# Retention products of three heads from fp32 to three fp32r passes, with split values and split decayed scores

## The chip, the cores and the metric

The kernel runs on one core of a Trainium2 chip. The metric is the device time of one execution in microseconds (us), the median of several runs. The engines are named as in the profile: PE is TensorE (matmuls), PEld its weight loads, DVE is VectorE, ACT is ScalarE, POOL is GpSimd, and SP issues most of the DMAs.

## The reference

Two transformer blocks one after the other, on 256 tokens of x and 256 of a context, width 1024. The first block's first layer is the one that matters here, retention with 4 heads (key width 256, value width 512), forwards and backwards. It is a scan over chunks of 128 tokens:

```
def step(r, qkv):
    qc, kc, vc = qkv
    s = einsum('bhid,bhjd->bhij', qc, kc) * dmask
    o = einsum('bhij,bhjv->bhiv', s, vc) + einsum('bhid,bhdv->bhiv', qc, r) * xi
    r = r * chunk_decay + einsum('bhjd,bhjv->bhdv', kc * zeta, vc)
    return r, o
...
ox_f, _ = retention_scan(qx, kx, vx, lg_f, rc_f)
ox_b, _ = retention_scan(flip(qx), flip(kx), flip(vx), lg_b, rc_b)
y = silu(gf) * head_norm(of) + silu(gb) * head_norm(ob)
return y @ w_out
```

All is float32. After it come a gated convolutional FFN, a layer of differential attention with another FFN, and a second block (two kinds of attention, a recurrent branch, an MLP).

## The kernel before

**Dense steps.** Nearly all of PE's work is weights times activations at nearly fp32 precision. A weight unit is 128 x 1024 numbers; four units (j = 0 to 3) make a step. SP loads a unit into `raw`; ScalarE copies it as fp32r into `wh` (L1619), VectorE makes `wl` = raw - wh (L2415), and PE runs three fp32r passes for each product, high x high, high x low and low x high (`three`, L615 to L617). A step is 4 units of 8 products of 512 columns, so 24 passes a unit. PE frees a unit by `unit_used`; ScalarE waits for that before it writes the next high part there. The results stand in half of PSUM (`main`, banks 0 to 3, or `side`, banks 4 to 7).

**Retention.** The scan is unrolled: all 512 tokens at once, four key tiles of 128. For each head h there are four dense steps, in this order: qk (queries and keys), v (values), gf and gb (the gates of both directions). Other work is hosted between the units of these steps, in the half of PSUM that the step does not use:
- v step: the queries and keys are turned (L921). At its end both engines copy the values to `vres`, ScalarE banks 0 and 1 (L1872) and VectorE banks 2 and 3 (L2788).
- gf step (here called the decay step): the scores (`score_tiles`, L930), tiles 0 to 2 after unit 0 and tile 3 after unit 1. VectorE multiplies them with decay factors from PSUM into `pf` and `pb`, forward and backward, 1280 columns each (`decay`, L2731).
- gb step: the forward products, decayed scores times values (`attend`, L937), 7 after unit 0 and 3 after unit 1.
- qk step of the next head: the backward products, also 7 and 3. (For the last head they lie between the first units of the output projection.)

Each `attend` is followed by ScalarE's squares (`rms_attended`, L1816, L1819) and VectorE's gate (`gate`, L2741 to L2749), and the next `attend` of the same direction waits for `gated`, since it writes the same banks. `silu_gate` (L1839) takes the gates out of PSUM at the end of gf and gb steps.

**Order.** Each engine's program is written out by hand, in the order in which it runs, and joined by semaphores. `close()` on VectorE waits for ScalarE's `act_evac` and then issues a tiny memset (L2437) that counts `emptied`: the half of PSUM is free. Between all this VectorE does `sum_slot` (L2477, L2479), the sums of modulation weights that POOL loads.

**Memory.** `pf` and `pb` lie in the arena at 32 and 37 kB, the turned queries and keys `qkt` at 42 to 50 kB, the decay factors `dec` at 58 to 62 kB. `ah` and `al` are the high and low activations for later projections; nothing uses them before the last head's retention.

Of the kernel before, what the change touches and what calls it, by code (L numbers as in the profile page):

```python
# [8 lines left out]
ALU = mybir.AluOpType  # L9
# [3 lines left out]
F32R = mybir.dt.float32r  # L13
# [170 lines left out]
def build(nc, a, out):  # L184
    ctx = ExitStack()
    with ctx:
        def sb(name, shape, dt=F32):
            return ctx.enter_context(nc.sbuf_tensor(name, shape, dt))

        def sem(name):  # L190
            return ctx.enter_context(nc.semaphore(name))
# [32 lines left out]
        spare = sb("spare", [1, 1])  # L224
        ARENA = 79 * 256
        arena = sb("arena", [P, ARENA])
        ps = ctx.enter_context(nc.psum_tensor("ps", [P, 8, 512], F32))

        def area(kb, *shape):

            n = int(np.prod(shape))
            o = int(kb * 256)
            assert o + n <= ARENA, (kb, shape)
            v = arena[:, o:o + n]
            if len(shape) == 1:
                return v
            names = "abcd"[:len(shape)]
            return v.rearrange(f"p ({' '.join(names)}) -> p {' '.join(names)}",
                               **dict(zip(names[1:], shape[1:])))
# [3 lines left out]
        qk = area(32, 4, 512)  # L243
        pf, pb = area(32, 1280), area(37, 1280)
        qkt = area(42, 4, 512)
        rtmp = area(42, 512)
        sgb = area(50, 4, 512)
        dec = area(58, 2, 512)
# [148 lines left out]
        y_rms, y_gated, h_done = sem("y_rms"), sem("y_gated"), sem("h_done")  # L397
        qkt_turned, qkt_act, qkt_vec = sem("qkt_turned"), sem("qkt_act"), sem("qkt_vec")
        scored, decayed = sem("scored"), sem("decayed")
        attended, gate_rms, gated = sem("attended"), sem("gate_rms"), sem("gated")  # L400
        y_turned, yt_act, yt_vec = sem("y_turned"), sem("yt_act"), sem("yt_vec")
        ada_summed, ada_added, mods_kept = sem("ada_summed"), sem("ada_added"), sem("mods_kept")
# [199 lines left out]
        def _(pe):  # L602
# [330 lines left out]
            def attend(v0, reads, tiles, half):  # L933

                for t in tiles:
                    for n, (c, k) in enumerate(reads[t]):
                        mm = pe.matmul(ps[:, half + t % 2, :], v0[:, c:c + P], vres[:, k, :],  # L937
                                       start=n == 0, stop=n == len(reads[t]) - 1)
                mm.then_inc(attended, 1)

            def turn_y(pair, half):

                for f in range(4):
                    for t in range(2):
                        c = (f % 2) * SEQ + t * P
                        mm = pe.transpose(ps[:, half + f // 2, c:c + P], sgf[:, 2 * pair + t, f * P:(f + 1) * P], ident[:, :])
                mm.then_inc(y_turned, 1)
# [11 lines left out]
            for h in range(RH):  # L959
                d = 4 * h  # L960
                dense = G.now() if h else 6
                if h:
                    mods_emptied(2 * h - 2)
                    pe.wait_ge(gated, 4 * h - 2)
                    for j in dense_tokens(main):
                        if j == 0:
                            pe.wait_ge(emptied, dense)
                            attend(pb, BWD_READS, (0, 1), side)
                        elif j == 1:
                            pe.wait_ge(gated, 4 * h - 1)  # L970
                            attend(pb, BWD_READS, (2, 3), side)
                        elif j == 2:
                            turn_y(0, side + 2)
                if h:
                    y_taken(2 * h - 1)
                    pe.wait_ge(gated, 4 * h)
                else:
                    pe.wait_ge(ada_taken, 4)
                    pe.wait_ge(emptied, 6)
                for j in dense_tokens(side):  # L980
                    if j == 0:
                        pe.wait_ge(emptied, dense + 1)
                        if h:
                            turn_y(1, main)
                    elif j == 1:
                        if h:
                            y_taken(2 * h)
                        pe.wait_ge(qk_rot, h + 1)
                        turn_q(h, 0, main)
                    elif j == 2:  # L990
                        qkt_taken(2 * h + 1)
                        turn_q(h, 1, main)
                    host_mods(d + 1, j, main)
                if h:
                    mods_emptied(2 * h - 1)
                qkt_taken(2 * h + 2)
                for j in dense_tokens(main):
                    if j == 0:
                        pe.wait_ge(emptied, dense + 2)
                        score_tiles((0, 1, 2), side)  # L1000
                    elif j == 1:
                        pe.wait_ge(decayed, 3 * h + 1)
                        score_tiles((3,), side)
                pe.wait_ge(decayed, 3 * h + 3)
                for j in dense_tokens(side):
                    if j == 0:
                        pe.wait_ge(emptied, dense + 3)
                    host_mods(d + 3, j, main)
                    if j == 0:
                        attend(pf, FWD_READS, (0, 1), main)  # L1010
                    elif j == 1:
                        pe.wait_ge(gated, 4 * h + 1)
                        attend(pf, FWD_READS, (2, 3), main)


            def project_rows(half, part):
# [586 lines left out]
        def _(act):  # L1603
# [238 lines left out]
            for h in range(RH):  # L1842
                def ahead(units):
                    split(units=units) if h < RH - 1 else split_rows(0, 0, units)

                if h:
                    silu_gate(sgb)
                    split(units=range(3, 4))
                    split(units=range(0, 1))
                    rms_attended(4 * h - 2, side)  # L1850
                    split(units=range(1, 2))
                    rms_attended(4 * h - 1, side)
                    split(units=range(2, 3))
                    take_y(2 * h - 2, side + 2)
                hb = step_full()
                T.mark(act.activation(qk[:, 2:4, :], ps[:, hb + 2:hb + 4, :], ACT.Copy), act_evac)
                split(units=range(3, 4))
                for z in range(2):
                    T.mark(act.activation(dec[:, z, :], kdist[:, z, :], ACT.Exp,
                                          scale=lgt[:, 4, h + 4 * z:h + 4 * z + 1]), (act_own, decay_exp)[z])  # L1860
                split(units=range(0, 1))
                if h:
                    take_y(2 * h - 1, main)
                    keep_mods(2 * h - 1, main)
                split(units=range(1, 2))
                take_qkt(2 * h, main)
                split(units=range(2, 3))
                take_qkt(2 * h + 1, main)
                if 2 * h - 1 in GATES:
                    keep_gate(2 * h - 1, main)  # L1870
                hb = step_full()
                T.mark(act.activation(vres[:, 0:2, :], ps[:, hb:hb + 2, :], ACT.Copy), act_evac)  # L1872
                split(units=range(3, 4))
                split(units=range(0, 3))
                silu_gate(sgf)
                split(units=range(3, 4))
                ahead(range(0, 1))
                keep_mods(2 * h, main)
                rms_attended(4 * h, main)
                ahead(range(1, 2))  # L1880
                rms_attended(4 * h + 1, main)
                ahead(range(2, 3))
                if 2 * h in GATES:
                    keep_gate(2 * h, main)
# [519 lines left out]
        def _(vec):  # L2404
# [15 lines left out]
            def step_full():  # L2420
                half = 4 * (par.base % 2)
                par.next()
                T.settle()
                vec.wait_ge(unit_used, S.next() * SLOTS + SLOTS)
                return half
# [13 lines left out]
            def act_read():  # L2439

                vec.wait_ge(act_evac, E.next() + 1)

            def close():

                act_read()
                tick(emptied)
# [35 lines left out]
            def sum_slot(d, j):  # L2482


                if 0 < d < 15:
                    sum_unit(4 * (d - 1) + j)
# [266 lines left out]
            for h in range(RH):  # L2753
# [31 lines left out]
                split(units=range(2, 3))  # L2785
                sum_slot(d + 1, 3)
                hb = step_full()
                T.mark(vec.tensor_copy(vres[:, 2:4, :], ps[:, hb + 2:hb + 4, :]), vec_own)  # L2788
                close()
                split(units=range(3, 4))  # L2790
                sum_slot(d + 2, 0)
                split(units=range(0, 1))
# [8 lines left out]
                sum_slot(d + 2, 2)  # L2801
                split(units=range(2, 3))
                sum_slot(d + 2, 3)
                step_full()
                close()
                split(units=range(3, 4))
# [805 lines left out]
```

## Time and profile before

| | |
|---|---|
| median of 3 runs | 1842.75 us (1841.95 to 1844.41) |
| the profiled execution | 1843.4 us, span 1841.3 us |
| granted clock, mean over the span | 0.992 |
| PE busy | 1789.2 us, 97% |
| VectorE busy | 1149.2 us, 62% |
| ScalarE busy | 837.7 us, 45% |
| DMA | 282.38 MB, mean 153 GB/s |

The span runs from the first to the last instruction; the execution's own time is a little longer. A busy share is an average over stages that have different limits. A matmul's record lasts longer than its slot in the stream, because matmuls overlap; the distance of two starts tells what one costs. The retention stage lies between about 60 and 520 us.

### The profile page before, as it was taken

How to read it: one execution, taken by the hardware profiler on the slowest of the kernel's cores; microseconds unless marked ns; L12 is line 12 of the kernel's file. 1: busy time of each engine (PE TensorE's matmuls, PEld its weight loads, DVE VectorE, ACT ScalarE, POOL GpSimd, SP SyncE). 2: the span in 40 equal slices, each digit the busy share in tenths (PEclk: the TensorE clock that was granted, in tenths of full speed). 3: DMA queues.
4: the chain of work that ended last, by engine and by line, in shares of the span. 5: the costliest groups of instructions: out<-in, count | busy, mean ns of one | idle time of the engine just before them, and what ended most of it. 6: DMA issues, size and time to landing. Idle time of an engine off the chain costs nothing. (4 is left out here: it accounts for less than half of the span.)

```text
span 1841.3 us, 26290 instructions
## 1 busy us (share of the span) xinstructions
PE 1789.2 (97%) x9881; PEld 1499.7 (81%) x9881; DVE 1149.2 (62%) x1539; ACT 837.7 (45%) x1216; POOL 85.4 (5%) x160
## 2 busy tenths in 40 slices
PE   7999999999999999999999998899999999989998
PEld 6877868778678888888878887799879987879987
DVE  4766667667267688644346566666665695765555
ACT  5334233241456432233345556566554646544454
POOL 3010101100000010000000000000001000000000
PEclk9999999999999999999999999999999999999999
DMA  9644545545265476432323222455546454536664
GB/s 333 207 134 147 167 142 157 154 125 174 85 225 184 132 233 184 127 105 81 114 68 104 81 81 81 139 181 182 192 141 209 148 165 144 188 126 194 182 194 126
DMA packets 153229, 282.38 MB, mean 153 GB/s; under 512 B 12795, under 2 KB 82547, under 8 KB 153008
## 3 DMA queue, kind: packets, MB, share of 16 engines
q1 hardware_dynamic: 136496, 223.69, 38.5%
q0 software_dynamic: 16640, 57.42, 10.3%
q8 instruction: 63, 1.03, 0.2%
q14 instruction: 30, 0.25, 0.0%
HBM read 276.83 MB, written 4.23 MB: 153 GB/s over the span
## 5 line engine op out<-in xcount | busy, mean ns | idle before, releaser
L2415 DVE TENSOR_TENSOR wl<-raw,wh 128x1024 fp32r<-128x1024 f32 (+1 forms) x388 | 455.1, 1181 | 377.2 <-ACT wh L1619 374.7
L1619 ACT ACTIVATE wh<-raw 128x1024 fp32r<-128x1024 f32 (+1 forms) x388 | 394.2, 1022 | 610.3 <-PE ps L617 603.2
L615 PE MATMUL ps<-uh,wh 128*128 128x256 f32 (+1 forms) x1216 | 382.2, 314 | 7.0 <-DVE spare L2437 7.0
L616 PE MATMUL ps<-ul,wh 128*128 128x256 f32 (+1 forms) x1216 | 380.2, 313 | 0.0
L617 PE MATMUL ps<-uh,wl 128*128 128x256 f32 (+1 forms) x1216 | 379.9, 312 | 0.0
L615 PE MATMUL ps<-wh,uh 128*128 128x512 f32 (+2 forms) x960 | 367.2, 382 | 7.1 <-issue 6.2
L616 PE MATMUL ps<-wl,uh 128*128 128x512 f32 (+2 forms) x960 | 353.5, 368 | 0.0
L617 PE MATMUL ps<-wh,ul 128*128 128x512 f32 (+2 forms) x960 | 353.3, 368 | 0.0
L615 PEld LDWEIGHTS ps<-uh,wh 128*128 128x128 f32 x1216 | 232.9, 192 | 22.4 <-issue 6.6
L617 PEld LDWEIGHTS ps<-uh,wl 128*128 128x128 f32 x1216 | 232.9, 192 | 12.5
L616 PEld LDWEIGHTS ps<-ul,wh 128*128 128x128 f32 x1216 | 233.0, 192 | 12.3
L615 PE MATMUL ps<-wh,ah 128*128 128x512 f32 x584 | 229.3, 393 | 0.6 <-DVE al L2550 0.4
L617 PE MATMUL ps<-wh,al 128*128 128x512 f32 x584 | 227.4, 389 | 0.0
L616 PE MATMUL ps<-wl,ah 128*128 128x512 f32 x584 | 227.3, 389 | 0.0
L615 PEld LDWEIGHTS ps<-wh,uh 128*128 128x128 f32 x960 | 182.1, 190 | 51.4 <-issue 20.3
L616 PEld LDWEIGHTS ps<-wl,uh 128*128 128x128 f32 x960 | 182.1, 190 | 33.3 <-issue 5.3
L617 PEld LDWEIGHTS ps<-wh,ul 128*128 128x128 f32 x960 | 181.7, 189 | 30.6
L2477 DVE SCALAR_TENSOR_TENSOR arena<-arena,cvec 128x1024 f32<-128x1024 f32 x140 | 173.6, 1281 | 8.4 <-DVE res L2749 0.5
L615 PEld LDWEIGHTS ps<-wh,ah 128*128 128x128 f32 x584 | 109.6, 188 | 26.0 <-issue 3.2
L617 PEld LDWEIGHTS ps<-wh,al 128*128 128x128 f32 x584 | 109.6, 188 | 22.9
L616 PEld LDWEIGHTS ps<-wl,ah 128*128 128x128 f32 x584 | 109.7, 188 | 22.7 <-issue 0.5
L937 PE MATMUL ps<-res,arena 128*128 128x512 f32 x160 | 72.5, 600 | 3.0 <-DVE res L2749 2.1
(315 smaller groups left out, 1491.5 us busy)
## 6 DMA issues: line engine op xcount, KB each, us to landing
raw<-in_ffn_w_up SPq DMA_DIRECT2D x176, 256.0 KB
arena<-in_ada_w POOLq DMA_DIRECT2D x80, 512.0 KB, 4.2
raw<-in_w_in SPq DMA_DIRECT2D x60, 512.0 KB
raw<-in_ret_w_in SPq DMA_DIRECT2D x48, 512.0 KB
raw<-in_ffn_w_down SPq DMA_DIRECT2D x40, 512.0 KB
raw<-in_ret_w_out SPq DMA_DIRECT2D x32, 512.0 KB
raw<-in_w_up SPq DMA_DIRECT2D x32, 512.0 KB
raw<-in_w_down SPq DMA_DIRECT2D x32, 512.0 KB
```

Of the source, the lines that this page charges most:

```text
L615: pe.matmul(o, lh, rh, start=first, stop=False)
L616: pe.matmul(o, lh, rl, start=False, stop=False)
L617: return pe.matmul(o, ll, rh, start=False, stop=last)
L937: mm = pe.matmul(ps[:, half + t % 2, :], v0[:, c:c + P], vres[:, k, :], start=n == 0, stop=n == len(reads[t]) - 1)
L1619: T.mark(act.activation(wh[:, j, 0:size], raw[:, j, 0:size], ACT.Copy), hi_done)
L2415: T.mark(vec.tensor_tensor(wl[:, j, 0:size], raw[:, j, 0:size], wh[:, j, 0:size], ALU.subtract), lo_done)
L2477: ins = vec.scalar_tensor_tensor(out=o, in0=w, scalar=c32[:, k, c:c + 1], in1=o, op0=ALU.mult, op1=ALU.add)
```

## The change

For heads 0 to 2 the values and the decayed scores are kept as a high part (fp32r) and a low part (the rest, as fp32r), and each product of `attend` becomes three fp32r passes (`attend_split`). Head 3 keeps the fp32 products, since `ah` and `al` are needed for the projection by then.

- Values: ScalarE writes the high part of all four banks to `ah` in two copies, VectorE subtracts twice into `al`. The copy to `vres` goes.
- Decayed scores: after the last decay ScalarE copies `pf` to `pfh` (1280 columns) and `pb` to `pbh` (768 and 512), between the high parts of units 1 and 2; VectorE subtracts in place to `pfl` and `pbl`, after its last sums and before the `close()` of the gf step. `pfh` and `pbh` lie where `qkt` and one half of `dec` have been.
- Four semaphores are new: v_high, v_low, p_high, p_low.

```diff
+        arena0 = nc.sbuf_base - 4 * ARENA
+        def split_area(name, kb, n):
+            return nc.alloc_sbuf_tensor_at(name, [P, n], F32R, offset=arena0 + 1024 * kb)
...
+        pfl, pbl = split_area("pfl", 32, 1280), split_area("pbl", 37, 1280)
+        pfh, pbh = split_area("pfh", 42, 1280), (split_area("pbh0", 47, 768), split_area("pbh1", 58, 512))
...
+            def attend_split(h, z, reads, tiles, half):
+                pe.wait_ge(v_low, h + 1)
+                pe.wait_ge(p_low, 2 * h + z + 1)
+                for t in tiles:
+                    for n, (c, k) in enumerate(reads[t]):
+                        if z == 0:
+                            ph = pfh[:, c:c + P]
+                        else:
+                            ph = pbh[0][:, c:c + P] if c < 768 else pbh[1][:, c - 768:c - 768 + P]
+                        mm = three(ps[:, half + t % 2, :], ph, (pfl, pbl)[z][:, c:c + P], ah[:, k, :], al[:, k, :],
+                                   n == 0, n == len(reads[t]) - 1)
+                mm.then_inc(attended, 1)
...
-                            attend(pb, BWD_READS, (0, 1), side)
+                            attend_split(h - 1, 1, BWD_READS, (0, 1), side)
...
-                        attend(pf, FWD_READS, (0, 1), main)
+                        if h < RH - 1:
+                            attend_split(h, 0, FWD_READS, (0, 1), main)
+                        else:
+                            attend(pf, FWD_READS, (0, 1), main)
...
-                T.mark(act.activation(vres[:, 0:2, :], ps[:, hb:hb + 2, :], ACT.Copy), act_evac)
+                if h < RH - 1:
+                    T.mark(act.activation(ah[:, 0:2, :], ps[:, hb:hb + 2, :], ACT.Copy), v_high)
+                    T.mark(act.activation(ah[:, 2:4, :], ps[:, hb + 2:hb + 4, :], ACT.Copy), act_evac)
+                else:
+                    T.mark(act.activation(vres[:, 0:2, :], ps[:, hb:hb + 2, :], ACT.Copy), act_evac)
                 split(units=range(3, 4))
-                split(units=range(0, 3))
+                split(units=range(0, 2))
+                if h < RH - 1:
+                    act.wait_ge(decayed, 3 * h + 3)
+                    T.mark(act.activation(pfh[:, :], pf, ACT.Copy), p_high)
+                    T.mark(act.activation(pbh[0][:, :], pb[:, 0:768], ACT.Copy), act_own)
+                    T.mark(act.activation(pbh[1][:, :], pb[:, 768:1280], ACT.Copy), p_high)
+                split(units=range(2, 3))
                 silu_gate(sgf)
...
-                T.mark(vec.tensor_copy(vres[:, 2:4, :], ps[:, hb + 2:hb + 4, :]), vec_own)
-                close()
+                if h < RH - 1:
+                    vec.wait_ge(v_high, h + 1)
+                    T.mark(vec.tensor_tensor(al[:, 0:2, :], ps[:, hb:hb + 2, :], ah[:, 0:2, :], ALU.subtract), vec_own)
+                    act_read()
+                    T.mark(vec.tensor_tensor(al[:, 2:4, :], ps[:, hb + 2:hb + 4, :], ah[:, 2:4, :], ALU.subtract), v_low)
+                    tick(emptied)
+                else:
+                    T.mark(vec.tensor_copy(vres[:, 2:4, :], ps[:, hb + 2:hb + 4, :]), vec_own)
+                    close()
...
                 sum_slot(d + 2, 3)
+                if h < RH - 1:
+                    vec.wait_ge(p_high, 2 * h + 1)
+                    T.mark(vec.tensor_tensor(pfl[:, :], pf, pfh[:, :], ALU.subtract), p_low)
+                    vec.wait_ge(p_high, 2 * h + 2)
+                    T.mark(vec.tensor_tensor(pbl[:, 768:1280], pb[:, 768:1280], pbh[1][:, :], ALU.subtract), vec_own)
+                    T.mark(vec.tensor_tensor(pbl[:, 0:768], pb[:, 0:768], pbh[0][:, :], ALU.subtract), p_low)
                 step_full()
                 close()
```

On PE, in the gb step of head 0 after unit 0, stood this. L879 are small fp32 matmuls of the modulation, and the row of L937 stands for 7 products:

```order
L617 MATMUL ps<-wh,ul 128x512
L879 MATMUL ps<-arena,pick 32x256 [waits ada_summed,emptied]
L879 MATMUL ps<-arena,pick 32x256 x7
L937 MATMUL ps<-res,arena 128x512 x7
L615 MATMUL ps<-wh,uh 128x512 [waits lo_done]
```

and now stands this, of which the last three rows come seven times (lines below the inserted ones have higher numbers):

```order
L625 MATMUL ps<-wh,ul 128x512
L887 MATMUL ps<-arena,pick 32x256 [waits ada_summed,emptied]
L887 MATMUL ps<-arena,pick 32x256 x7
L623 MATMUL ps<-ah,pfh 128x512 [waits p_low,v_low]
L624 MATMUL ps<-al,pfh 128x512
L625 MATMUL ps<-ah,pfl 128x512
```

The block keeps its place behind the small matmuls; it has 21 passes for 7 products and waits for both low parts.

On VectorE, in the gf step of head 0 from the last decay to the low part of unit 3, stood this:

```order
L2731 SCALAR_TENSOR_TENSOR arena<-ps,arena 128x256 x2
L2477 SCALAR_TENSOR_TENSOR arena<-arena,cvec 128x1024 [waits decayed,ada_loaded0]
L2477 SCALAR_TENSOR_TENSOR arena<-arena,cvec 128x1024
L2415 TENSOR_TENSOR wl<-raw,wh 128x1024 [waits hi_done]
L2477 SCALAR_TENSOR_TENSOR arena<-arena,cvec 128x1024 [waits lo_done,ada_loaded1]
L2477 SCALAR_TENSOR_TENSOR arena<-arena,cvec 128x1024
L2437 MEMSET spare 1x1 [waits act_evac,ada_summed,unit_used]
L2415 TENSOR_TENSOR wl<-raw,wh 128x1024 [waits hi_done] x2
```

and now, from the sums on:

```order
L2454 TENSOR_TENSOR wl<-raw,wh 128x1024 [waits hi_done]
L2516 SCALAR_TENSOR_TENSOR arena<-arena,cvec 128x1024 [waits lo_done,ada_loaded1]
L2516 SCALAR_TENSOR_TENSOR arena<-arena,cvec 128x1024
L2852 TENSOR_TENSOR pfl<-arena,pfh 128x1280 [waits p_high]
L2854 TENSOR_TENSOR pbl<-arena,pbh_53 128x512 [waits p_high]
L2855 TENSOR_TENSOR pbl<-arena,pbh_52 128x768
L2476 MEMSET spare 1x1 [waits act_evac,p_low,unit_used]
L2454 TENSOR_TENSOR wl<-raw,wh 128x1024 [waits hi_done] x2
```

Three subtractions stand between the last sums and the memset that frees the half of PSUM. In the same step ScalarE's program had, from the high part of unit 1 on:

```order
L1619 ACTIVATE wh<-raw 128x1024 [waits unit_used,raw_loaded1]
L1619 ACTIVATE wh<-raw 128x1024 [waits unit_used,raw_loaded2]
L1839 ACT_TABLE_LOAD [waits unit_used]
L1839 ACTIVATE res<-ps 128x2048 [waits hi_done]
L1619 ACTIVATE wh<-raw 128x1024 [waits unit_used,raw_loaded3]
```

and has:

```order
L1648 ACTIVATE wh<-raw 128x1024 [waits unit_used,raw_loaded1]
L1910 ACTIVATE pfh<-arena 128x1280 [waits decayed]
L1911 ACTIVATE pbh_52<-arena 128x768
L1912 ACTIVATE pbh_53<-arena 128x512
L1648 ACTIVATE wh<-raw 128x1024 [waits unit_used,raw_loaded2]
L1868 ACT_TABLE_LOAD [waits unit_used]
L1868 ACTIVATE res<-ps 128x2048 [waits hi_done]
```

Three copies stand between the high parts of units 1 and 2, behind a wait for the last decay.

## Rows read from the trace of the kernel before

Times in a timeline are us from the start of the span; a bracket at the end of a row is the idle time of that engine before it, and what ended it. PEld is the weight load of TensorE.

**Rows 1.** The page: busy time, share and instructions of each engine.
```profile
PE 1789.2 (97%) x9881; PEld 1499.7 (81%) x9881; DVE 1149.2 (62%) x1539; ACT 837.7 (45%) x1216; POOL 85.4 (5%) x160
```

**Rows 2.** Windows, head 1's decay step: PE, PEld, DVE, ACT, POOL busy; PEclk, DMA, GB/s.
```profile
198.00:225.00 27.00, 27.00 (x114) 21.04 (x112) 20.04 (x28) 5.14 (x5) 2.30 (x5) 1.00 0.51 161
```

**Rows 3.** The page: costliest groups, the fp32 products with values.
```profile
L937 PE MATMUL ps<-res,arena 128*128 128x512 f32 x160 | 72.5, 600 | 3.0 <-DVE res L2749 2.1
```

**Rows 4.** Timeline of PE in a dense step: start us, us, instruction.
```profile
172.05 0.39 PE L615 MATMUL ps<-wh,uh 128*128 128x512 f32 x1
...
177.26 0.39 PE L617 MATMUL ps<-wh,ul 128*128 128x512 f32 x1
```

**Rows 5.** Timeline of PE, head 0's backward blocks: ends of their neighbours.
```profile
145.12 0.40 PE L617 MATMUL ps<-wh,ul 128*128 128x512 f32 x1
...
151.60 0.40 PE L616 MATMUL ps<-wl,uh 128*128 128x512 f32 x1
...
157.54 2.84 PE L937 MATMUL ps<-res,arena 128*128 128x512 f32 x6 [0.53 <-DVE res L2749]
...
160.45 0.39 PE L616 MATMUL ps<-wl,uh 128*128 128x512 f32 x1
```

**Rows 6.** Timeline of PE, head 0's forward blocks, then L879 with no block behind.
```profile
114.24 6.28 PE L937 MATMUL ps<-res,arena 128*128 128x512 f32 x14
...
120.59 0.39 PE L616 MATMUL ps<-wl,uh 128*128 128x512 f32 x1
...
126.19 2.82 PE L937 MATMUL ps<-res,arena 128*128 128x512 f32 x6
...
129.08 0.40 PE L616 MATMUL ps<-wl,uh 128*128 128x512 f32 x1
...
179.46 0.50 PE L615 MATMUL ps<-wh,uh 128*128 128x512 f32 x1
...
179.80 0.40 PE L616 MATMUL ps<-wl,uh 128*128 128x512 f32 x1
```

**Rows 7.** Timeline of VectorE, v and decay steps of head 0; last, a backward gate.
```profile
82.95 1.22 DVE L2415 TENSOR_TENSOR wl<-raw,wh 128x1024 fp32r<-128x1024 f32 x1 [0.59 <-ACT wh L1619]
...
87.49 1.23 DVE L2415 TENSOR_TENSOR wl<-raw,wh 128x1024 fp32r<-128x1024 f32 x1 [0.72 <-ACT wh L1619]
...
89.86 2.34 DVE L2731 SCALAR_TENSOR_TENSOR arena<-ps,arena 128x256 f32<-128x256 f32 x8 [0.75 <-PE ps L930]
...
96.42 1.23 DVE L2415 TENSOR_TENSOR wl<-raw,wh 128x1024 fp32r<-128x1024 f32 x1 [1.62 <-ACT wh L1619]
...
97.56 1.28 DVE L2731 SCALAR_TENSOR_TENSOR arena<-ps,arena 128x256 f32<-128x256 f32 x4
...
103.62 1.23 DVE L2415 TENSOR_TENSOR wl<-raw,wh 128x1024 fp32r<-128x1024 f32 x1 [2.19 <-ACT wh L1619]
...
104.95 2.48 DVE L2477 SCALAR_TENSOR_TENSOR arena<-arena,cvec 128x1024 f32<-128x1024 f32 x2
...
111.35 0.06 DVE L2437 MEMSET spare<- 1x1 f32 x1 [3.92 <-ACT res L1839]
...
154.62 0.17 DVE L2741 RECIPROCAL st<-st 128x2 f32<-128x2 f32 x1 [1.52 <-ACT st L1819]
```

**Rows 8.** Timeline of ScalarE in the same two steps.
```profile
80.95 1.03 ACT L1872 ACTIVATE res<-ps 128x1024 f32<-128x1024 f32 x1 [4.80 <-PE ps L617]
...
102.53 1.06 ACT L1619 ACTIVATE wh<-raw 128x1024 fp32r<-128x1024 f32 x1 [6.14 <-PE ps L617]
...
109.25 1.88 ACT L1839 ACTIVATE res<-ps 128x2048 f32<-128x2048 f32 x1
```

**Rows 9.** Timeline of PE: first scores, and first small matmuls of the gb step.
```profile
86.14 3.61 PE L930 MATMUL ps<-arena 128*128 128x256 f32 x12
...
113.24 1.07 PE L879 MATMUL ps<-arena,pick 128*32 128x256 f32 x16
```

**Rows 10.** Groups by form: VectorE's low part of 512 columns.
```profile
L2415 DVE TENSOR_TENSOR wl<-raw,wh 128x512 fp32r<-128x512 f32 x24 | 16.4, 689 | 16.0 <-ACT wh L1619 15.7
```

More of the change, by code:

```diff
@@ L399, in build @@
         scored, decayed = sem("scored"), sem("decayed")
+        v_high, v_low, p_high, p_low = sem("v_high"), sem("v_low"), sem("p_high"), sem("p_low")
         attended, gate_rms, gated = sem("attended"), sem("gate_rms"), sem("gated")
@@ L967, in _ @@
                             pe.wait_ge(emptied, dense)
-                            attend(pb, BWD_READS, (0, 1), side)
+                            attend_split(h - 1, 1, BWD_READS, (0, 1), side)
                         elif j == 1:
                             pe.wait_ge(gated, 4 * h - 1)
-                            attend(pb, BWD_READS, (2, 3), side)
+                            attend_split(h - 1, 1, BWD_READS, (2, 3), side)
                         elif j == 2:
@@ L1009, in _ @@
                     if j == 0:
-                        attend(pf, FWD_READS, (0, 1), main)
+                        if h < RH - 1:
+                            attend_split(h, 0, FWD_READS, (0, 1), main)
+                        else:
+                            attend(pf, FWD_READS, (0, 1), main)
                     elif j == 1:
                         pe.wait_ge(gated, 4 * h + 1)
-                        attend(pf, FWD_READS, (2, 3), main)
+                        if h < RH - 1:
+                            attend_split(h, 0, FWD_READS, (2, 3), main)
+                        else:
+                            attend(pf, FWD_READS, (2, 3), main)
             def project_rows(half, part):
@@ L2787, in _ @@
                 hb = step_full()
-                T.mark(vec.tensor_copy(vres[:, 2:4, :], ps[:, hb + 2:hb + 4, :]), vec_own)
-                close()
+                if h < RH - 1:
[4 more added lines that the diff above has]
+                    tick(emptied)
+                else:
+                    T.mark(vec.tensor_copy(vres[:, 2:4, :], ps[:, hb + 2:hb + 4, :]), vec_own)
+                    close()
                 split(units=range(3, 4))
@@ L2803, in _ @@
                 sum_slot(d + 2, 3)
+                if h < RH - 1:
+                    vec.wait_ge(p_high, 2 * h + 1)
[3 more added lines that the diff above has]
+                    T.mark(vec.tensor_tensor(pbl[:, 0:768], pb[:, 0:768], pbh[0][:, :], ALU.subtract), p_low)
                 step_full()
```

## The prediction

> **What bounds the kernel now.** I read the page's busy times first: PE works 97% of the span, and no other engine comes near [rows 1]. Then the windows of the retention stage: in the 27 us of head 1's decay step PE is busy for 27.00, at a granted clock of 1.00 (the 2.4 GHz level), with VectorE at 20.04, ScalarE at 5.14 and the DMA engines at half of their time [rows 2]. The reader is to see that in this stage a microsecond taken from PE's stream is a microsecond off the time, as long as the other two engines keep delivering what PE is about to need. So three questions remain: how long the changed products take on PE, whether the added work of VectorE and ScalarE fits into their idle time, and whether an earlier end of retention reaches the end of the kernel.
>
> **PE's part.** A head has 10 products forwards (7 hosted after unit 0 of a step, 3 after unit 1) and 10 backwards (7 and 3). The fp32 product is two records; there are 160 of them, so 80 products, and 60 belong to the three heads that change [rows 3].
>
> The new price: in a dense step an fp32r pass of 512 columns follows the one before at a fixed pitch. From the L615 at 172.05 to the L617 at 177.26 are 23 passes, 5.21 us, so 0.2265 us a pass [rows 4]. Three passes make 0.68 us a product, 4.76 us for 7 and 2.04 us for 3.
>
> The old price, read as the time that a block adds to the stream between two fp32r passes:
> - backward 7: from the L617 at 145.12 to the L616 at 151.60 are 6.48 us. Without a block there would be two pitches, 0.45, so it adds 6.03 us [rows 5]. Gain 6.03 - 4.76 = 1.27.
> - forward 7: from 114.24 to the L616 at 120.59 are 6.35 us [rows 6]. Where the same small fp32 matmuls (L879) are followed by no block, L615 to L616 takes 0.34 (179.46 to 179.80) [rows 6]; so 6.01 us. Gain 1.25.
> - forward 3: 126.19 to 129.08, 2.89 - 0.34 = 2.55 us [rows 6]. Gain 0.51.
> - backward 3: 157.54 to 160.45, 2.91 us, less one pass of 0.23 to 0.34, about 2.63 us [rows 5]. Gain 0.59.
>
> Together 3.62 us a head, times three heads: **10.9 us**. This includes the pause at each change from fp32 to fp32r, which goes where both neighbours are fp32r. Bounds: if each of the 12 blocks keeps a pause of 0.11 us (0.34 - 0.23), the gain is 9.6. If the busy time of the fp32 group is the true price, 72.5 / 80 = 0.906 us a product [rows 3], it is 60 x (0.906 - 0.68) = 13.6. I take 10.9, since the blocks were measured in their places.
>
> The row speaks of 0.2265 us a pass, each with its own weight load. The Trainium skill (TensorE: Matmul & The Clock Gate, Back-to-back issue gap) puts a stream of weight loads and 512-column matmuls at about 131 ns each; by that the product would fall to 0.39 us and the 60 products would give back some 28 us. This trace does not agree: its stream of just that kind runs at 0.2265.
>
> **The wait for the backward 3** stays. PE stands 0.53 us by the bracket [rows 5] until the gate of the first pair is done (L2749). That chain starts at the last matmul of the 7, and PE's cover for it (the units of j = 1, 24 passes) starts there too; both move together. VectorE must be at its place: it enters the gate at 154.62 after waiting 1.52 us [rows 7]. The block ends 1.27 us earlier after the change while VectorE's sums before it do not move, which leaves 0.25 us of that wait. So no loss, but narrowly; each 0.1 us beyond would cost 0.1 on three blocks.
>
> **VectorE and ScalarE at the end of the v step.** Now: both engines copy half of the values from 80.95 on, ScalarE for 1.03 us [rows 8], and VectorE reaches unit 3's low part at 82.95 [rows 7]. After: ScalarE's first high copy to about 82.0, VectorE's subtraction (as L2415 of the same width, 1.23 us) to 83.3, the second to 84.5, then the memset that ends the group, about 84.6. PE asks for it at 86.14, ahead of the scores [rows 9]: 1.5 us to spare. VectorE is then some 1.7 us later than before. It idled 0.59, 0.72 and 0.75 us before 82.95, 87.49 and 89.86 [rows 7]; the first goes, the second and third swallow 1.47, so the decays start 0.2 to 0.4 us late, and the idle 1.62 before 96.42 [rows 7] closes it. The tile-3 scores come 5.4 us of matmuls after the first, against 2.34 us of decays, so they do not wait.
>
> **The split of the decayed scores.** The last decay ends at 97.56 + 1.28 = 98.84 [rows 7]. ScalarE then waits for it and makes three copies of 1280, 768 and 512 columns. By the 1.06 us of a 1024-column copy [rows 8] in proportion they take 2.65 us; with a fixed part in each, up to 3.0. Done at 101.5 to 101.9, while the copy queued behind it (high part of unit 2) starts at 102.53, when PE frees the unit [rows 8]. Slack 0.6 to 1.0 us. VectorE comes free at 104.95 + 2.48 = 107.43 [rows 7] and subtracts three times. 512 columns take 0.69 us and 1024 take 1.23 [rows 7, 10], so 1280 about 1.50 and 768 about 0.96: 3.15 us, or about 2.9 as they overlap by some 0.1. Done by 110.4. The memset that releases the group stood at 111.35, behind the 3.92 us that VectorE waited for ScalarE's silu (109.25 + 1.88) [rows 7, 8]. So that wait hides it, with 0.8 us over. PE first needs the release at 113.24 and the low parts at 114.24 [rows 6, 9]: even without the cover of the silu VectorE could be 2.7 us late before PE stood. Behind the memset are the low parts of units 3 and 0 of the next weights, needed a whole step later. Cost: nothing. The three heads have the same pattern.
>
> POOL and SP issue no DMA more or less, and their transfers wait for the same events.
>
> **Sum.** Against the profiled execution (1843.4 us, span 1841.3): 1843.4 - 10.9 = 1832.5. Its time is 0.65 above the median of the runs, 1842.75; from that I forecast **1832 us**.
>
> **Rivals.**
> 1. *Full gain, as above.* 0.73. Its own range is the bounds 9.6 and 13.6 off, with the 1.2 us by which the runs differ from each other: 1828 to 1834.
> 2. *A part is eaten by new waits*: VectorE is late at the gate of the backward 3 and at the releases. For: only 0.25 us of slack at the gate, 0.8 in the split. Against: everything else has more. If the gates come 0.5 us late on the three blocks and the releases 0.5 us on six, 4.5 us go: 1836. Up to 9 us gone, if they come 1 us late. 0.12.
> 3. *The passes of a block run slower than in a dense step.* This is the one on the other side. Twelve passes in a row go into one PSUM bank, where the dense steps change bank after three. Break-even is 6.03 / 21 = 0.287 us a pass. If the next pass had to await the end of the one before, whose record takes 0.39 us, a product would cost 1.17 and the 60 would add 60 x (1.17 - 0.86) = 18.6 us: 1861. Against: the fp32 records go up to eight into one bank, 14 in 6.28 us [rows 6], below the 0.592 us that each lasts, so they overlap. 0.05.
> 4. *The gain does not reach the end*: a later stage hangs on a transfer that comes no earlier. Then 1843. For: PE is idle for some 52 us of the span. Against: the weights are loaded into slots that PE frees, so they move along. 0.05.
> 5. *Deeper overlap of passes in a block*: were a pass only as long as its weight load, 0.19 us, the 60 products would cost 0.57 each and the gain would be 60 x (0.86 - 0.57) = 17: 1825. Nothing in the rows speaks for it; the skill's rate, above, would go further in the same direction. 0.02.
> 6. *Work moved by 11 us meets other clock windows.* The granted clock over the whole execution is 0.992, so somewhere after retention it was at the 1.2 GHz level for short stretches. More or fewer of them could change the time by 3 us either way: 1829 to 1835 about my value. 0.03.
>
> **How the numbers follow.** A measurement here can tell 0.2%, 3.7 us. Cases 1, 5, 6 and most of 2 are faster: 0.73 + 0.02 + 0.03 + 0.10 = 0.88. Within 0.2%: the rest of 2 and case 4: 0.07. Slower: 0.05. The range 1828 to 1837 takes case 1, case 6 and the half of 2 that loses up to 5 us: about 0.82.
>
> **What would show it.** In the changed trace: blocks of 21 and 9 passes at 0.2265 us; no idle of PE ahead of the forward blocks, and about 0.5 us, as now, ahead of the backward 3; ScalarE's copies of the decayed scores over before PE frees unit 2; the memset after the gf step still released by silu; the retention stage some 11 us shorter and the stages after it as long as before. Wrong would be: a pitch above 0.23 in the blocks, or PE waiting for v_low, p_low or a release.

## The result and the profile after

The median of 7 runs is **1836.0 us** (1832.99 to 1837.22), beside 1844.71 for 7 runs of the kernel before that were taken on the same chips. The ratio is 0.9947, with a 95% interval of 0.9938 to 0.9957: some 10 us less, with an interval of 8 to 11. The forecast was 1832, the range 1828 to 1837. One run of a kernel below took 1934.37 us at a granted clock of 0.893; its ratio leaves that run out.

The profiled execution took 1837.22 us, the longest of the seven, with a span of 1835.1 and a mean granted clock of 0.991. The profiled execution of the kernel before (1843.4 us, clock 0.992) was shorter than the median there, so the two spans differ by 6.2 us only. From its page, the row that answers to [rows 1]; behind it, from the groups of TensorE's instructions by form, one of the six groups of new passes:

```profile
PE 1781.3 (97%) x9941; PEld 1512.6 (82%) x9941; DVE 1160.4 (63%) x1551; ACT 847.7 (46%) x1228; POOL 85.4 (5%) x160
...
L624 PE MATMUL ps<-al,pfh 128*128 128x512 f32 x30 | 11.8, 394 | 0.0
```

TensorE gives up 7.9 us of busy time. VectorE and ScalarE each take on 10 to 11 us, spread over three heads.

Where did the time go? The program of TensorE is the same outside the blocks, so the starts of the same instruction can be compared along it. This is TensorE's timeline in head 0, the forward blocks (answers to [rows 6]):

```profile
113.65 1.07 PE L887 MATMUL ps<-arena,pick 128*32 128x256 f32 x16
114.65 0.51 PE L623 MATMUL ps<-ah,pfh 128*128 128x512 f32 x1
114.99 0.39 PE L624 MATMUL ps<-al,pfh 128*128 128x512 f32 x1
...
119.89 0.40 PE L624 MATMUL ps<-wl,uh 128*128 128x512 f32 x1
```

and these are the backward blocks (answer to [rows 5]), with the same place of head 2 at the end:

```profile
143.92 0.40 PE L625 MATMUL ps<-wh,ul 128*128 128x512 f32 x1
...
149.26 0.39 PE L624 MATMUL ps<-wl,uh 128*128 128x512 f32 x1
...
155.20 0.50 PE L623 MATMUL ps<-ah,pbh 128*128 128x512 f32 x1 [0.57 <-DVE res L2788]
...
385.96 0.39 PE L624 MATMUL ps<-wl,uh 128*128 128x512 f32 x1
```

In the kernel before, the instruction that answers to the last row started here:

```profile
395.29 0.39 PE L616 MATMUL ps<-wl,uh 128*128 128x512 f32 x1
```

The stretch from the first small matmuls of head 0 to this place held 12 blocks: 395.29 - 113.24 = 282.05 us before, 385.96 - 113.65 = 272.31 after. The three heads give **9.74 us**, 3.25 each. In it the forward 7 gave 6.35 - (119.89 - 114.65) = 1.11 us and the backward 7 gave 6.48 - (149.26 - 143.92) = 1.14. The new passes do not run at the dense pitch, the 0.2265 us between two starts in a dense step [rows 4]: from 114.99 to 119.89 are 21 pitches in 4.90 us, 0.233 each, and the backward stretch has 23 in 5.34, 0.232.

The waits of TensorE from 100 to 400 us have a single row, three times 0.57 us ahead of the backward 3:

```profile
PE ps L623 <- DVE res L2788: 1.7, 3, 0.6
```

**The added work.** VectorE's timeline in head 0 (answers to [rows 7]), then ScalarE's (answers to [rows 8]). All starts are 0.41 us later than in the kernel before, by a shift that lies ahead of the change.

```profile
82.52 1.23 DVE L2829 TENSOR_TENSOR al<-ps,ah 128x1024 fp32r<-128x1024 f32 x1 [2.28 <-ACT ah L1902]
...
84.92 0.06 DVE L2476 MEMSET spare<- 1x1 f32 x1
...
90.29 2.34 DVE L2770 SCALAR_TENSOR_TENSOR arena<-ps,arena 128x256 f32<-128x256 f32 x8
...
97.97 1.28 DVE L2770 SCALAR_TENSOR_TENSOR arena<-ps,arena 128x256 f32<-128x256 f32 x4
...
109.76 0.95 DVE L2855 TENSOR_TENSOR pbl<-arena,pbh 128x768 fp32r<-128x768 f32 x1
111.76 0.06 DVE L2476 MEMSET spare<- 1x1 f32 x1 [1.05 <-ACT res L1868]
...
152.28 0.17 DVE L2780 RECIPROCAL st<-st 128x2 f32<-128x2 f32 x1 [0.38 <-ACT st L1848]
```

```profile
101.19 0.61 ACT L1912 ACTIVATE pbh<-arena 128x512 fp32r<-128x512 f32 x1
102.94 1.06 ACT L1648 ACTIVATE wh<-raw 128x1024 fp32r<-128x1024 f32 x1 [1.13 <-PE ps L625]
...
109.65 1.88 ACT L1868 ACTIVATE res<-ps 128x2048 f32<-128x2048 f32 x1
```

Take 0.41 off each start. The decays begin at 89.88 (89.86 before) and the last ends at 98.84, to the hundredth as before; VectorE's idle stretches had swallowed the longer v step (those of 0.59, 0.72 and 0.75 us in [rows 7] are gone). The copies are done at 101.39, 1.13 us before ScalarE can go on. The subtractions end at 110.30, and the memset stands at 111.35, where it stood before, still released by silu.

**After retention.** TensorE had 0.29 us of idle ahead of a group of the next stage before, waiting for `al`. After, in this execution (TensorE's waits from 395 to 620 us):

```profile
PE ps L790 <- DVE arena L2542: 1.6, 2, 1.3
PE ps L623 <- DVE al L2589: 1.2, 1, 1.2
```

Before, the same two waits were 1.0 and 0.4 us in all, so 1.4 us of the 9.7 are lost here. They come with a burst of transfers: in the window from 520 to 530 us the DMA share is 1.02 at 398 GB/s, and two engines wait for loads (waits by DMA, same stretch):

```profile
DVE arena L2914 <- DMA arena<-in_norm_g: 5.3, 1, 5.3
ACT wh L1708 <- DMA raw<-in_ret_w_out: 2.7, 2, 1.7
ACT wh L1648 <- DMA raw<-in_ffn_w_up: 2.3, 1, 2.3
```

The kernel before had only the first of these, 4.4 us, though its burst was as dense (1.02 at 413 GB/s from 530 to 540 us). Whether that belongs to the change is what the first and the fourth kernel below ask.

From 385.96 us to the end of the span are 1449.1 us, from 395.29 in the kernel before 1446.0: 3.1 us more, in a part of the program where TensorE's instructions are the same. Nearly half of it are the waits just named. The other half came between 960 and 1200 us, where the trace has 20.5 us at the 1.2 GHz level, and 17.1 us before. With the shift of 0.41 ahead of retention the account closes: 9.74 - 3.1 - 0.41 = 6.2 us, the difference of the spans.

### The profile page after: what moved, and what is told of

Same layout as the page of the kernel before. It is cut to its first block and busy times, and to the rows that moved or that the text cites. A ratio compares the mean times of both kernels' runs of the same rounds, so it can differ in the third digit from the quotient of the medians.

```text
span 1835.1 us, 26443 instructions
## 1 busy us (share of the span) xinstructions
PE 1781.3 (97%) x9941; PEld 1512.6 (82%) x9941; DVE 1160.4 (63%) x1551; ACT 847.7 (46%) x1228; POOL 85.4 (5%) x160
## 5 line engine op out<-in xcount | busy, mean ns | idle before, releaser
L623 PE MATMUL ps<-wh,uh 128*128 128x512 f32 (+2 forms) x960 | 362.1, 377 | 7.1 <-issue 6.2
L3589 POOL DMA_DIRECT2D arena<-in_ada_w x80 | 42.4, 530 | 564.9 <-DVE arena L2516 338.3
```

The source lines that it names most:

```text
L623: pe.matmul(o, lh, rh, start=first, stop=False)
L3589: pool.dma_start(aring[:, u % 2, :], a["ada_w"][l].rearrange("(k p) n -> k p n", p=P)[k][:, n * D:(n + 1) * D]).then_inc(ada_loaded[u % 2] ...
```

## The experiments

The kernels of each group below shared their runs of the kernel before. Those medians were 1843.64 (15 runs; the first four kernels), 1843.54 (18 runs; the next four) and 1844.44 (9 runs; the last).

**The changed kernel again**, with no edit.

> The changed kernel once more, to see what of its trace repeats. Theory 1 (the gain is the shorter products alone, and what is missing is given back to transfers after retention): 9 to 11 us below the kernel before; up to 396 us PE's stream is again 9.7 us ahead, and the waits for in_norm_g (5.34 us on VectorE) and for weights after retention (2.7 and 2.3 us on ScalarE) come back within 0.5 us. Theory 2 (those waits are chance): the same time, but they are as in the kernel before, 4.44 us and none.

Measured: 1836.92 us, ratio 0.996 (0.9946 to 0.9974). TensorE's timeline at the two ends of the retention stretch:

```profile
114.90 1.07 PE L887 MATMUL ps<-arena,pick 128*32 128x256 f32 x16
...
387.19 0.39 PE L624 MATMUL ps<-wl,uh 128*128 128x512 f32 x1
```

That is 272.29 us, beside 272.31: the 9.7 us repeat. The waits behind it do not. The two of TensorE are 1.0 and 0.5 us in all, as in the kernel before, and no weight load is waited for by ScalarE. Behind the stretch are 1447.6 us, 1.5 less than in the first execution. Still the span (1834.8 us, clock 0.989) is hardly shorter, as retention began 1.25 us later (114.90 for 113.65): between 20 and 40 us this execution has 6.8 us at the 1.2 GHz level, the first has none. So the transfer waits vary from one execution to the next; they are no cost that the change brings each time.

**The added work alone.** All copies, subtractions and semaphores stay, but the products of the three heads are the old fp32 ones, on tiles that the split does not fill (so the values and scores in these products are not the head's own).

```diff
-                        mm = three(ps[:, half + t % 2, :], ph, (pfl, pbl)[z][:, c:c + P], ah[:, k, :], al[:, k, :],
-                                   n == 0, n == len(reads[t]) - 1)
+                        mm = pe.matmul(ps[:, half + t % 2, :], kret[:, c:c + P], vres[:, k, :],
+                                       start=n == 0, stop=n == len(reads[t]) - 1)
```

> All of the split's work (ScalarE's copies, VectorE's subtractions, PE's waits for v_low and p_low) stays, but PE makes the old fp32 products, on constants and stale values in place of the decayed scores and values. Theory 1: the work is hidden, so the time is that of the kernel before, within 1.5 us. Rival (the work costs something, and the passes alone would bring more): 2 to 5 us above the kernel before.

Measured: 1844.1 us, ratio 1.0002 (0.9992 to 1.0011). TensorE's timeline:

```profile
113.44 1.07 PE L887 MATMUL ps<-arena,pick 128*32 128x256 f32 x16
...
395.46 0.39 PE L624 MATMUL ps<-wl,uh 128*128 128x512 f32 x1
```

282.02 us, beside 282.05 before. The some 21 us that VectorE and ScalarE work more cost nothing in retention, and nothing in the whole time that these runs could tell (the interval is 1.5 us less to 2.0 us more).

**The passes alone.** Values and scores are written once, as fp32r, and the same tile serves as high and as low part; nothing is split (the products are not the sum of high and low parts).

```diff
+                        p, v = (pfr, pbr)[z][:, c:c + P], vresr[:, k, :]
+                        mm = three(ps[:, half + t % 2, :], p, p, v, v, n == 0, n == len(reads[t]) - 1)
```

> The kernel before, with three fp32r passes for a product in heads 0 to 2, but without any split: values and decayed scores are rounded once where they are written anyway, and the same operand serves for the high and the low part. Theory 1: as the changed kernel, 9 to 10.5 us below the kernel before. Rival (the split's work costs something): 12 us or more below.

Measured: 1833.85 us, ratio 0.9949 (0.9936 to 0.9963). TensorE's timeline:

```profile
113.28 1.07 PE L882 MATMUL ps<-arena,pick 128*32 128x256 f32 x16
...
385.83 0.40 PE L619 MATMUL ps<-wl,uh 128*128 128x512 f32 x1
```

272.55 us, beside 272.31 for the whole change. Together with the kernel before it this shows where the time of the stretch comes from: all of it from the passes, none lost to the split. The median is 3 us below the 1836.92 of the changed kernel that ran beside it, but the intervals of the two ratios overlap, and the profiled execution had only 23.9 us at the 1.2 GHz level between head 3's end and its last matmul, where that of the changed kernel had 30.7. A loss to the split of a microsecond or two outside retention is neither shown nor excluded.

**The gates of the next stage later**, to take VectorE's wait for `in_norm_g` off its queue.

```diff
-            take_gates(4, 3)
             split_rows(1, 0, range(4))
+            take_gates(4, 3)
```

> The changed kernel, with VectorE's multiplication of the gates by the norm's gain (the one that waits for in_norm_g) moved behind the low parts of the next four units. Theory 1 (that wait delays the low parts, and PE with them): PE's 1.19 us of idle before the second projection goes, and the time is 1 to 1.5 us below the changed kernel, 10.5 to 12 below the kernel before. Rival (the low parts would be late anyway, as ScalarE waits for the same transfers): no gain on the changed kernel, the idle stays.

Measured: 1835.58 us, ratio 0.9958 (0.9944 to 0.9972), no different from the changed kernel. The wait for `in_norm_g` is gone from VectorE. But TensorE idles all the same, a little later in its program (its timeline), and ScalarE waits for a weight unit (waits by DMA):

```profile
550.66 0.47 PE L623 MATMUL ps<-wh,ah 128*128 128x512 f32 x1 [1.19 <-DVE al L2589]
```

```profile
ACT wh L1708 <- DMA raw<-in_ret_w_out: 2.8, 2, 1.4
```

The burst holds some engine up in this execution too, only another one; taking one reader of it off the path earned nothing that can be seen.

**One pass fewer.** The third pass of each product, low scores times high values, is left out of the sum.

```diff
-                        mm = three(ps[:, half + t % 2, :], ph, (pfl, pbl)[z][:, c:c + P], ah[:, k, :], al[:, k, :],
-                                   n == 0, n == len(reads[t]) - 1)
+                        o = ps[:, half + t % 2, :]
+                        pe.matmul(o, ph, ah[:, k, :], start=n == 0, stop=False)
+                        mm = pe.matmul(o, ph, al[:, k, :], start=False, stop=n == len(reads[t]) - 1)
```

> The changed kernel without the third pass of each of the 60 products (the low part of the decayed scores times the high part of the values is left out of the sum, so the retention output is less exact); everything else stays, the low parts of the scores are still made and waited for. Theory 1, retention is bound by TensorE's stream and each pass in a block costs its pitch, 0.233 us as read in the changed kernel's trace: 60 x 0.233 = 14.0 us less than the changed kernel. What could eat a part: the backward block of 7 ends 1.6 us earlier, but VectorE's sums before the gate do not move, so the wait before the backward block of 3 should grow from about 0.6 us by up to 1.4 us a head, 4 us in all. So 10 to 14 us below the changed kernel: 1822 to 1826 beside 1836. Rival, the stream is bound by something else by now (the deliveries of VectorE and ScalarE at the gates): the time falls by less than 6 us and all the waits ahead of the blocks grow.

Measured: 1823.94 us, ratio 0.9886 (0.9872 to 0.9901), 12 us below the changed kernel. TensorE's timeline, the ends of the stretch and the first backward 3:

```profile
114.93 1.07 PE L887 MATMUL ps<-arena,pick 128*32 128x256 f32 x16
...
153.68 0.50 PE L961 MATMUL ps<-ah,pbh 128*128 128x512 f32 x1 [1.73 <-DVE res L2789]
...
376.78 0.40 PE L624 MATMUL ps<-wl,uh 128*128 128x512 f32 x1
```

The stretch takes 261.85 us, 10.5 less. The 60 passes are worth 14.0, and the wait ahead of the backward 3 grew from 0.57 to 1.73 us, three times 1.16 = 3.5. The sum comes out at 10.5. A shorter block thus lengthens this wait once VectorE's 0.38 us of slack there are used up; the prediction's worry about the gate was right in kind. (The medians lie 12 us apart, the ratios 11; with four runs of this kernel that is not told from 10.5.)

**Two banks in turn.** The blocks change PSUM bank after every product.

```diff
-                for t in tiles:
-                    for n, (c, k) in enumerate(reads[t]):
+                for n in range(max(len(reads[t]) for t in tiles)):
+                    for t in tiles:
+                        if n >= len(reads[t]):
+                            continue
+                        c, k = reads[t][n]
```

> The blocks of the changed kernel take their two tiles in turn, so that the PSUM bank changes after every product (three passes) instead of after nine or twelve; the same 21 and 9 passes, the same sums. Theory 1: the pitch of 0.233 us inside a block, against 0.2265 us in a dense step, comes from the many passes into one bank; then a block of 21 passes takes 4.76 us instead of 4.90 and the 180 passes give 180 x 0.0065 = 1.2 us: 0.9993 of the changed kernel, 0.9940 beside before instead of 0.9947. Rival: the pitch has another cause (the values and scores lie elsewhere, as does the order of weights), or is the mean of three passes of unlike kind, and the block stays at 4.90 us, with no difference in time.

Measured: 1836.28 us, ratio 0.9957 (0.9945 to 0.9969). TensorE's timeline:

```profile
115.07 0.39 PE L624 MATMUL ps<-al,pfh 128*128 128x512 f32 x1
...
119.96 0.40 PE L624 MATMUL ps<-wl,uh 128*128 128x512 f32 x1
```

21 pitches in 4.89 us, 0.233, as with one bank. The bank is not the cause. Nor are the split tiles: with the passes alone, above, seven pitches of the last block (383.73 to 385.37 us) are 0.234 each. What the cause is stays open.

**VectorE later by one instruction, and by three**, ahead of the subtractions from the backward scores (an in-place maximum of the scores with themselves). This is the edit with one; the other has 3 in its place.

```diff
+                    for _ in range(1):
+                        T.settle()
+                        T.mark(vec.tensor_tensor(pb, pb, pb, ALU.max), vec_own)
+                    T.settle()
```

> The changed kernel with one more instruction on VectorE in the decay step of each of the three heads: an in-place maximum over the 1280 columns of the backward decayed scores (it changes no number), about 1.4 us, ahead of their two subtractions. Theory 1 (slack): the memset that frees the half of PSUM moves from 111.76 to about 112.2 us in head 0, still before the 113.65 us at which TensorE asks for it; nothing waits, and the time is that of the changed kernel, 1835 to 1837. Rival (this place has already no room, and part of what the change gives is lost here): 1.4 us a head, 4 us in all: 1840.

Measured: 1836.13 us, ratio 0.9959 (0.9944 to 0.9974). No loss shows; the only wait of TensorE in the stage is the old one. VectorE's timeline shows the memset right behind the last subtraction now, with silu's cover used up:

```profile
110.89 0.95 DVE L2859 TENSOR_TENSOR pbl<-arena,pbh 128x768 fp32r<-128x768 f32 x1
111.99 0.06 DVE L2476 MEMSET spare<- 1x1 f32 x1 [0.15 <-DVE pbl L2859]
```

TensorE asks for it at 113.05 in this execution. Against that moment the subtractions end 1.73 us later than in the changed kernel (111.84, 1.21 ahead of it, for 110.71, 2.94 ahead of 113.65), and the memset comes 0.83 us later; silu's cover was the 0.9 us between.

> The same with three such instructions in each of the three heads, about 4.2 us more on VectorE. Theory 1 (slack): the memset comes at 115.0 to 115.4 us in head 0, TensorE asks for it at 113.65 us, so it stands 1.4 to 1.7 us in each head, 4 to 5 us in all: 1840 to 1841. Rival (no room at all): 4.2 us x 3 = 12.6 us, 1848. Rival (the wait is caught up later, since VectorE is not the engine that bounds): 1836.

Measured: 1843.58 us, ratio 0.9995 (0.9985 to 1.0005): the whole gain is gone, 7.5 us above the kernel with one instruction, where 4 to 5 were expected. VectorE's timeline, and TensorE's behind it:

```profile
109.00 4.54 DVE L2856 TENSOR_TENSOR arena<-arena 128x1280 f32<-128x1280 f32 x3
...
115.29 0.06 DVE L2476 MEMSET spare<- 1x1 f32 x1 [0.15 <-DVE pbl L2859]
```

```profile
115.41 1.70 PE L887 MATMUL ps<-arena,pick 128*32 128x256 f32 x16 [2.03 <-DVE spare L2476]
117.04 0.80 PE L623 MATMUL ps<-ah,pfh 128*128 128x512 f32 x1
117.63 0.63 PE L624 MATMUL ps<-al,pfh 128*128 128x512 f32 x1
...
233.27 1.07 PE L887 MATMUL ps<-arena,pick 128*32 128x256 f32 x16 [2.03 <-DVE spare L2476]
```

The wait is 2.03 us a head, 6.1 in all, since TensorE asked at 113.38 and the memset came at 115.29. In head 0 more is lost behind it: the small matmuls take 1.70 us instead of 1.07 and a pass 0.63 instead of 0.39. The windows say why (busy time of PE, PEld, DVE, ACT, POOL; then the granted clock, DMA share, GB/s):

```profile
113.00:116.00 3.00, 0.97 (x10) 0.31 (x12) 2.81 (x5) 1.06 (x1) 0.00 (x0) 0.95 0.00 0
116.00:119.00 3.00, 3.00 (x17) 1.79 (x10) 2.86 (x4) 0.38 (x1) 0.00 (x0) 0.50 0.42 133
```

After the idle 2 us the engine ran at the 1.2 GHz level for about 3 us. In heads 1 and 2 the same wait was followed by windows with a clock of 1.00. What the level cost can be taken from the stretch of retention, which begins behind head 0's wait: 393.33 - 115.41 = 277.92 us here, 385.34 - 113.05 = 272.29 with one instruction. Of the 5.63 us the waits of heads 1 and 2 are 4.07, so 1.6 are left for the lower clock in head 0. A wait thus cost its own length, and in one of three heads 1.6 us on top: 6.1 + 1.6 = 7.7, beside the 7.5 of the medians. What was expected, 4 to 5 us, lacked the second part, and took the added work for 4.2 us a head where the subtractions ended 4.7 us later.

**Head 3 too.** Its high values go where its fp32 values were, the low ones into free room of the arena, and its 20 products become three passes each.

```diff
-                        if h < RH - 1:
-                            attend_split(h, 0, FWD_READS, (0, 1), main)
-                        else:
-                            attend(pf, FWD_READS, (0, 1), main)
+                        attend_split(h, 0, FWD_READS, (0, 1), main)
...
-                    attend(pb, BWD_READS, (0, 1), side)
+                    attend_split(RH - 1, 1, BWD_READS, (0, 1), side)
```

> The changed kernel with the same treatment for head 3: its high values in the area that held them as fp32, its low values in room of the arena that is free by then, and three fp32r passes for its 20 products too. Theory 1 (the gain is a fixed price a block, wherever it stands): head 3 gives what each of the others gave in the trace, 3.2 us, so 1833 beside 1836 for the changed kernel; ratio to before 0.9930 instead of 0.9947. Rival (head 3 is different: its backward blocks lie between the first units of the output projection, and the splits meet the work of the gates there): new waits of TensorE of 1 to 3 us, and the time is that of the changed kernel.

Measured: **1831.3 us** (1830.72 to 1834.81), ratio 0.9928 (0.9915 to 0.9942), the fastest with all three passes in place. From head 2's last block to head 3's last, on TensorE's timeline, first of this kernel, then of the changed one:

```profile
387.80 0.40 PE L626 MATMUL ps<-wl,uh 128*128 128x512 f32 x1
...
500.55 0.40 PE L626 MATMUL ps<-wl,ah 128*128 128x512 f32 x1
```

```profile
501.85 0.40 PE L624 MATMUL ps<-wl,ah 128*128 128x512 f32 x1
```

112.75 us beside 501.85 - 385.96 = 115.89: head 3 gives 3.14 us, and the two waits of its backward blocks (0.87 and 0.53 us) are as before.

In this execution the gain did not outlive the burst. VectorE waited 6.5 us for `in_norm_g` there, TensorE for VectorE, and behind that wait TensorE fell to the 1.2 GHz level (its timeline, then the window from 540 to 550 us, with a clock of 0.83):

```profile
540.05 0.49 PE L625 MATMUL ps<-wh,ah 128*128 128x512 f32 x1 [2.31 <-DVE al L2584]
```

```profile
540.00:550.00 10.00, 9.95 (x37) 8.08 (x38) 9.82 (x14) 6.36 (x14) 0.00 (x0) 0.83 0.65 210
```

From head 3's last block to one and the same later instruction are 552.64 - 500.55 = 52.09 us here, 551.55 - 501.85 = 49.70 in the changed kernel and 560.01 - 511.21 = 48.80 in the kernel before: the 3 us were given back. This was also the longest of the five executions, by 3.2 us; that the gain reaches the end in the others rests on their times alone, as they have no profile.

## Why the prediction was right, and where it was off

- **What bounds the kernel**: right. In retention a microsecond off TensorE's stream is one off the time (the passes alone, and one pass fewer), and 7.5 us are lost when TensorE is kept waiting 6.1.
- **PE's part**, predicted 10.9 us, with the bound 9.6: measured 9.74. The mis-sized term is the price of a pass, 0.2265 us taken from a dense step [rows 4]. In the blocks it is 0.2325 on average, 60 x 3 x 0.006 = 1.1 us, which is nearly the whole difference. The prediction named "a pitch above 0.23 in the blocks" as a sign of being wrong, and by its own sign this term was. The kernel before had a hint: behind its first forward block six dense passes, from 120.59 to 121.98 us, took 0.232 each. By the blocks, the forward 7 gave 1.11 (1.25 predicted), the backward 7 1.14 (1.27); the two blocks of 3 share the remaining 1.0 us of a head (1.10 predicted).
- **The wait before the backward 3** stays, 0.57 us for 0.53, with 0.38 us of slack at the gate where 0.25 was worked out. That this slack is narrow was shown by the kernel with one pass fewer.
- **The v step**: memset predicted at 84.6, it stood at 84.92, 84.51 without the shift of 0.41. The decays start where they did.
- **The split**: the subtractions were done at 110.30, for 110.4 predicted, the memset did not move, and the estimate that VectorE could be late by 0.8 us without any effect, and by 2.7 before TensorE stands, holds in both parts. With one instruction more the subtractions ended 1.73 us later and the memset 0.83, so the first room is 0.9; with three they ended 4.7 us later (115.14, for the 2.94 us ahead of TensorE's asking in the changed kernel 1.76 behind it), and TensorE stood 2.03, so the second is 2.7.
- **Rivals.** New waits (2): not in retention. Slower passes (3): true by 2.6%, far from the break-even at 0.287 us. Gain not reaching the end (4): most of it does, but in a single execution up to 1.5 us are given back at the burst of transfers, and 3.3 in the one of the kernel with head 3. Deeper overlap (5): no. By the Trainium skill (TensorE: Matmul & The Clock Gate, Back-to-back issue gap), with about 131 ns a matmul, it should have been far more; the trace of the change does not agree with it either, at 0.2325. Clock (6): the traces bear it out as a spread, not as a shift. The twelve executions of the changed kernel run from 1832.99 us at a granted clock of 0.993 to 1839.07 at 0.989, and the 49 of the kernel before from 1841.67 to 1849.85.
- **The number.** 1832 was 4 us low. 1.1 of it is the pitch. Some 1.3 is the base: 1842.75 was the median of 3 runs, and the median of all 49 runs of the kernel before is 1844.0. The rest, some 1.6 us, lies behind retention or in the noise. The 49 runs of the kernel before have a mean of 1844.3 us, the 33 runs of the six kernels whose stream is as short in retention (the changed one, again, passes alone, gates later, two banks, one instruction more) one of 1835.8: 8.5 less, with a standard error of 0.4, where retention gives 9.7. In the traces, from the end of the stretch to the end of the span, these six have between 1445.6 and 1449.1 us, on average 1447.5; the two executions with fp32 products have 1446.0 and 1448.9. So no steady loss shows there, and one of a microsecond is not excluded. That 1836.0 lies in the range is owed to the range's width as well as to the mechanism.

## What to carry to other kernels

When an engine's stream is the bound, price the new instructions in a place like the one where they will stand, and take the stretch between two fixed neighbours, not the records: it holds the pauses too. Then look up for each added instruction what idle time hides it and how much of that is left; here adding work on purpose, once below and once above the room that had been worked out, confirmed the figure. The price of a wait can be more than its length, though, when the clock falls behind it. And what works for three of four equal parts is worth trying on the fourth: the room for its low parts was there, and gave 3 us in the stream and 3.5 by the ratios.

## What was not expected of the hardware

- An fp32r pass of 512 columns has a pitch of 0.232 to 0.233 us in these blocks (and in the few passes behind one) and 0.2265 in a dense step, with the same instruction and a weight load each, and not because of the bank.
- A wait of 2.03 us was followed by some 3 us at the 1.2 GHz level in head 0 and by none in heads 1 and 2, in one execution.
- Whether a load of 256 or 512 KB is late in a burst (DMA share 0.98 to 1.02) differs between executions of the same program: ScalarE waited 5.0 us for weights in one and not at all in the next.
